# Pooled product gated in place, first pairs of the input and out projections in turns, VectorE's gates behind softmax scaling

## The reference

```python
h = rms_norm(x, norm_w)
proj = einsum('bld,dn->bln', h, w_in)      # 5824 columns: aq ak av ag bq bk bv bg cq ckv ckr cg du dg
ya = diff_attention(aq, ak, av, ...)       # 4 heads, two softmax maps per head, RMSNorm behind it
yb = axial_gqa(bq, bk, bv, ...)            # 4 query heads, 2 key heads
yc = latent_attention(cq, ckv, ckr, ...)   # cq and ckv normalised, then projected up
yd = multiscale_pool(du, w_group, scale)   # mean window minus token, per-group matmul, scale
y = concat(ya * silu(ag), yb * silu(bg), yc * silu(cg), yd * silu(dg))
x = x + einsum('bln,nd->bld', y, w_out)
```

## Time and profile before

| what | value |
|---|---|
| median of 3 runs | 952.94 us (951.38 to 953.1) |
| the profiled execution's own time | 950.87 us |
| its span | 948.8 us, 18299 instructions |
| TensorE matmul busy | 920.9 us (97%), 7138 instructions |
| TensorE weight load busy | 875.5 us (92%) |
| VectorE busy | 702.4 us (74%), 1130 instructions |
| ScalarE busy | 556.5 us (59%), 985 instructions |
| mean granted clock of TensorE | 0.994 |
| DMA | 143.97 MB, mean 152 GB/s |

### The profile page before, as it was taken

The page is one execution under the profiler, slowest core; times in us unless marked ns, Lnnn a source line. Parts: engine busy times, 40 slices in busy tenths (PEclk is TensorE's granted clock), DMA queues, the critical chain, the costliest instruction groups (busy, mean ns, idle before and its releaser), DMA issues.

```text
span 948.8 us, 18299 instructions
## 1 busy us (share of the span) xinstructions
PE 920.9 (97%) x7138; PEld 875.5 (92%) x7138; DVE 702.4 (74%) x1130; ACT 556.5 (59%) x985; POOL 0.2 (0%) x4
## 2 busy tenths in 40 slices
PE   8989999999999999999999989999999999989998
PEld 7988889998999998899999979999989998988998
DVE  7767987778797788876664568877787868787553
ACT  7667657658666565554544576666576565553331
POOL 0000000000000000000000000000000000000000
PEclk9999999999999999999999999999999999999999
DMA  9534332333333333245454343324334344335552
GB/s 357 224 127 181 131 133 90 135 133 134 134 134 136 132 134 133 89 179 178 179 189 179 134 178 134 134 102 166 134 134 178 115 154 159 138 111 200 194 177 90
DMA packets 22997, 143.97 MB, mean 152 GB/s; under 512 B 2560, under 2 KB 4608, under 8 KB 6528
## 3 DMA queue, kind: packets, MB, share of 16 engines
q1 hardware_dynamic: 22768, 142.77, 41.6%
q10 hardware_dynamic: 144, 0.04, 0.0%
HBM read 140.70 MB, written 2.10 MB: 151 GB/s over the span
## 4 chain that ended last, share of the span: by engine, by line
PE 73%; DVE 18%; ACT 7%; issue 2%; DMA 0%; ACTq 0%; DVEq 0%; SPq 0%
PE dense L671 21%; PE dense L673 21%; PE dense L672 21%; DVE w_lo L1250 5%; DVE c_st L1375 4%; PE o_ps L864 3%; PE s_ps L829 2%; ACT w_hi L954 2%; PE norm_ps L782 1%; PE t_ps L845 1%; DVE stat L1410 1%; ACT y_hi L1079 1%; ACT row L979 1%; DVE c_st L1374 1%; DVE row L1258 1%
## 5 line engine op out<-in xcount | busy, mean ns | idle before, releaser
L671 PE MATMUL dense<-h_hi,w_hi 128*128 128x272 f32 (+1 forms) x1472 | 438.3, 298 | 3.6 <-ACT row L979 1.8
L673 PE MATMUL dense<-h_hi,w_lo 128*128 128x272 f32 (+1 forms) x1472 | 422.6, 287 | 0.0
L672 PE MATMUL dense<-h_lo,w_hi 128*128 128x272 f32 (+1 forms) x1472 | 420.5, 286 | 0.0
L1250 DVE TENSOR_TENSOR w_lo<-raw,w_hi 128x1024 fp32r<-128x1024 f32 (+1 forms) x257 | 313.3, 1219 | 68.3 <-ACT w_hi L954 60.8
L954 ACT ACTIVATE w_hi<-raw 128x1024 fp32r<-128x1024 f32 (+1 forms) x257 | 271.3, 1056 | 69.3 <-PE dense L673 58.8
L671 PEld LDWEIGHTS dense<-h_hi,w_hi 128*128 128x128 f32 x1472 | 277.3, 188 | 10.8 <-issue 3.8
L672 PEld LDWEIGHTS dense<-h_lo,w_hi 128*128 128x128 f32 x1472 | 277.7, 189 | 1.4
L673 PEld LDWEIGHTS dense<-h_hi,w_lo 128*128 128x128 f32 x1472 | 277.0, 188 | 0.0
L671 PE MATMUL dense<-y_hi,w_hi 128*128 128x272 f32 (+1 forms) x564 | 163.6, 290 | 11.2 <-ACT row L979 7.1
L673 PE MATMUL dense<-y_hi,w_lo 128*128 128x272 f32 (+1 forms) x564 | 162.4, 288 | 0.0
L672 PE MATMUL dense<-y_lo,w_hi 128*128 128x272 f32 (+1 forms) x564 | 162.1, 287 | 0.0
(11 more groups left out here) (134 smaller groups left out, 707.0 us busy)
## 6 DMA issues: line engine op xcount, KB each, us to landing
raw<-w_stream_dram SPq DMA_DIRECT2D x128, 1024.0 KB, 4.8
out_dram<-x SPq DMA_DIRECT2D x8, 256.0 KB, 6.5
x<-xt_dram SPq DMA_DIRECT2D x3, 544.0 KB, 7.9
raw<-w_stream_dram SPq DMA_DIRECT2D x3, 512.0 KB, 7.2
con<-consts_dram SPq DMA_DIRECT2D x1, 984.0 KB, 13.4
x<-xt_dram SPq DMA_DIRECT2D x2, 272.0 KB, 4.6
raw<-w_stream_dram SPq DMA_DIRECT2D x2, 256.0 KB, 4.4
d_w<-consts_dram SPq DMA_DIRECT2D x2, 256.0 KB, 8.2
```

Source lines behind the costliest of these rows:

```text
L671: nc.tensor.matmul(ps, whi, xhi, start=first, stop=False)
L672: nc.tensor.matmul(ps, whi, xlo, start=False, stop=False)
L673: return nc.tensor.matmul(ps, wlo, xhi, start=False, stop=last)
L1250: signal(nc.vector.tensor_tensor(w_lo[:, g % RING, 0:n], raw[:, e % RAW, CHUNK * half:CHUNK * half + n], w_hi[:, g % RING, 0:n].bitcast(F3 ...
```

## The change

Six edits, all in the order of work and in which buffer or bank it uses; the matmuls are the same in number and shape.

1. Input pairs 0 and 1 of layer 0 and out pairs 0 and 1 of both layers are taken in turns: chunk b of pair 0, chunk b of pair 1, then b + 1. Since four tiles are then open, the tiles of the second pair lie in other banks (`side`): `t_ps` and `o_ps` at the start, `norm_ps` and `swap_ps` in the out projection.
2. At the start, x block 2 is loaded behind weight chunk 3 and x block 3 behind the next weights; constants and tables go three entries later; `x_first` stages stand later in the lists; the three lambda stages go from slots 8 to 10 to slots 13 to 15.
3. The `dg` gate writes its product in place, `c_st[:, i]`, and its `y_split` goes one slot later, with other offsets (ScalarE 0.77 to 0.23, VectorE 1.284 to 0.284).
4. VectorE's `gate` offset goes from 0.336 to 0.6.
5. `y_split` of ckv goes one slot later, the three stages of `kr` too.
6. `x_out` of pair 0 comes three slots later, where the pair now ends; layer 1's first lifts wait for the splits of layer 0's gated rows instead of for the gates.

```diff
+def pair_end(layer, p):
+    return 6 + p if layer == 0 and p < 2 else pair_slot(p) + 3
+
+def out_end(n):
+    return pair_slot(N_PAIRS) + (6 + n if n < 2 else 4 * n + 3)
...
-  AT_SCALAR:  y_gate=0.77
+  AT_SCALAR:  y_gate=0.23
-  AT_VECTOR:  gate=0.336, y_gate=1.284
+  AT_VECTOR:  gate=0.6, y_gate=0.284
...
     for s in range(1, AHEAD + 1):
-        plan += [(-10 + s, 0, ("split", 0, s)), (-10 + s, 1, ("x_first", 0, s))]
+        plan.append((-10 + 2 * s, 0, ("split", 0, s)))
+    plan += [(-5, 0, ("x_first", 0, 1)), (-3, 0, ("x_first", 0, 2)), (2.9, 0, ("x_first", 0, 3))]
...
             for n, stage in enumerate(("lam_dot", "lam_exp", "lam_out")):
-                at(8 + n, (stage, l))
+                at(13 + n, (stage, l))
...
                     if kind == "dg":
-                        at(s, ("y_split", "gate", l, kind, i0 + j, j))
+                        at(s + 1, ("y_split", "gate", l, kind, i0 + j, j))
...
-            at(s + n + 2, ("y_split", "lat_fin", l, key))
-        at(s + 3, ("rope_pre", l, "kr", 0, None))
-        at(s + 4, ("rope_stat", l, "kr", 0))
-        at(s + 5, ("rope_fin", l, "kr", 0))
+            at(s + 2 + 2 * n, ("y_split", "lat_fin", l, key))
+        at(s + 4, ("rope_pre", l, "kr", 0, None))
+        at(s + 5, ("rope_stat", l, "kr", 0))
+        at(s + 6, ("rope_fin", l, "kr", 0))
...
-    def chunk_kind(s):
+    def chunk_kind(l, s):
+        if l == 0 and s < 8:
+            return "in", s % 2, s // 2
...
-            return ("out", *divmod(s - pair_slot(N_PAIRS), 4))
+            n = s - pair_slot(N_PAIRS)
+            return ("out", n % 2, n // 2) if n < 8 else ("out", *divmod(n, 4))
...
+    def bank_of(tile):
+        if tile in side:
+            l, j = side[tile]
+            return (t_ps, o_ps)[j] if l is None else (norm_ps, swap_ps)[j]
+        return dense[tile % 2]
...
-            if e == 2:
+            if e == 2:
+                sp.dma_start(x[:, 12:16, :], xt[:, 12:16, :]).then_inc(s_x[3], 16)
+            if e == 5:
                 sp.dma_start(con[:, 0:N_MATS], consts[:, 0:N_MATS]).then_inc(s_const, 16)
-            if e == 3:
+            if e == 6:
...
         def bank_for(tile):
-            if tile >= 2:
-                kind, n = freed_by[tile - 2]
+            if tile in side:
+                l, j = side[tile]
+                if l is None:
+                    pass
+                elif j == 0:
+                    pe.wait_ge(rn_ready, 1 + max(n for st, n in norm_order.items() if st[1] == l))
+                else:
+                    last = [st for st in swap_list if st[1] == l][-1]
+                    pe.wait_ge(takes_swap[last[0]], swap_taken_value(last))
+            elif tile >= 2:
+                before_it = tile - 2 if tile - 2 not in side else tile - 4
+                kind, n = freed_by[before_it]
                 pe.wait_ge(taken[kind], n)
-            return dense[tile % 2]
+            return bank_of(tile)
...
-            signal(nc.vector.tensor_tensor(yt[:, t0:L], ta[:, t0:L], c_st[:, i, t0:L], ALU.mult), gate_done, n)
+            signal(nc.vector.tensor_tensor(c_st[:, i, t0:L], ta[:, t0:L], c_st[:, i, t0:L], ALU.mult), gate_done, n)
```

More of the change, by code:

```diff
@@ L108 @@
                  y_split=0.205, xscale=0.283, sub_pre=0.439, x_out=0.55, p_out=0.56, gate=0.574, s_exp=0.579,
-                 lift=0.6, up_out=0.705, split=0.71, x_square=0.72, y_gate=0.77, lam_exp=0.793, v_out=1.297)
+                 lift=0.6, up_out=0.705, split=0.71, x_square=0.72, y_gate=0.23, lam_exp=0.793, v_out=1.297)
 AT_VECTOR = dict(sq_sum=0.2, rope_mid=0.25, s_max=-0.418, lam_dot=-0.35, sub_fin=-0.345, rope_fin=-0.34, lat_fin=0.055, head_out=0.17,
-                 y_split=0.19, pool=0.266, xscale=0.283, gate=0.336, s_scale=0.491, x_out=0.512, rescale=0.55,
-                 x_add=0.614, split=0.71, lam_out=0.82, y_gate=1.284)
+                 y_split=0.19, pool=0.266, xscale=0.283, gate=0.6, s_scale=0.491, x_out=0.512, rescale=0.55,
+                 x_add=0.614, split=0.71, lam_out=0.82, y_gate=0.284)
 MOVED = {("split", 1, 56): 0.54, ("lift", 1, 2, 1): 0.49, ("lift", 0, 22, 0): -0.39, ("split", 1, 102): 0.87,
@@ L148, in make_plan @@
         for p, (kind, i0) in enumerate(PAIRS):
-            end = g0 + pair_slot(p) + 3
+            end = g0 + pair_end(l, p)
             for j in (0, 1):
@@ L219, in make_plan @@
         for n in range(O_PAIRS):
-            at(g0 + pair_slot(N_PAIRS) + 4 * n + 3, ("x_out", l, n))
+            at(g0 + out_end(n), ("x_out", l, n))
     return [("setup", 0)] + [stage for _, _, stage in sorted(plan)]
@@ L379, in build @@
     n_taken = {"in": 0, "up": 0, "out": 0}
-    freed_by, tile_no = {}, {}
+    freed_by, tile_no, side = {}, {}, {}
     n_tile = 0
@@ L393, in build @@
                 tile_no[(l, *m)] = n_tile
+                if m[0] == "out" and m[1] == 1:
+                    side[n_tile] = (l, m[2])
+                if l == 0 and m[0] == "in" and m[1] == 1:
+                    side[n_tile] = (None, m[2])
                 freed_by[n_tile] = (m[0], n_taken[m[0]])
@@ L557, in y_tile @@
             r = rows_of("d", source[3])
-            return n, lambda y: y[:, r, t0:L], yt[:, t0:L], (gate_done, gate_no[source])
+            return n, lambda y: y[:, r, t0:L], c_st[:, source[3], t0:L], (gate_done, gate_no[source])
         _, b, h, i = score_steps(l)[source[2]]
@@ L962, in lift @@
                 if l:
-                    act.wait_ge(gate_done, gates_of_layer * l)
+                    act.wait_ge(y_ready, max(y_count[(l - 1, 3, i)] for i in range(4)))
                 if kind == "cqr" and j and l:
@@ L1505, in add @@
             n += 1
-        for p in range(N_PAIRS):
+        for b in range(KT // CK) if l == 0 else ():
+            for p in (0, 1):
+                a = OFF[PAIRS[p][0]]
+                add(wi[CK * b:CK * b + CK, :, a:a + 256])
+        for p in range(2 if l == 0 else 0, N_PAIRS):
             kind, i = PAIRS[p]
@@ L1529, in pack_weights @@
                 n += 1
-        for p in range(O_PAIRS):
-            for b in range(KT // CK):
-                k = CK * OUT_ORDER[b]
-                add(wo[k:k + CK, :, 256 * p:256 * p + 256])
+        for p, b in ([(p, b) for b in range(KT // CK) for p in (0, 1)]
+                     + [(p, b) for p in range(2, O_PAIRS) for b in range(KT // CK)]):
+            k = CK * OUT_ORDER[b]
+            add(wo[k:k + CK, :, 256 * p:256 * p + 256])
     return stream.reshape(DEPTH * ENTRIES, 128, 2 * CHUNK)
```

16 lines of the change are left out of this document (9 added, 7 removed).

## The result

| | before | after |
|---|---|---|
| median (executions) | 951.92 us (14) | 955.83 us (15) |
| lowest and highest | 950.97 to 954.31 | 954.08 to 958.87 |
| profiled execution, span | 950.87, 948.8 | 956.15, 954.2 |
| all idle time ahead of matmuls | 24.2 us | 27.7 us |

The account below looks back on a forecast made before the run. TensorE was taken as the bound, its matmuls in flight 920.9 of 948.8 us. Start -1.5, up projection -3.7, out projection -2.8, gates +4.4 gave -3.6: 947.3 us, 949.3 on the median's scale; range from 944.0 to 954.0.

Parts of the forecast that it names:

- the gates: VectorE's gates pass s_scale and s_max, so other stages come later: loss 4.4 us, bounds 1.8 gain to 6 loss.
- the out projection: Pairs in turns: the last gated row is needed later, y_lo and x_out stalls go: gain 2.8 us (2.3 to 2.8).
- The start: Input pairs in turns: second chunk starts at about 10.9, fifth at 20.4: gain 1.5 us (1.0 to 2.0).
- The up projection: First up chunks: one long stall becomes two, clock kept in one layer of two: gain 3.7 us (1.8 to 5.6).
- rival 2: Lower clock stays behind both up projection stalls: 951.2 us, no difference that can be told; chance 0.23.
- Slot 93: Layer 0: s_max ahead of the gate makes it end at 383.9, y_split, p_out and pv follow: loss 2.0 us.
- Slot 95: Layer 0: a lift goes ahead of the y_split, so the 1.84 us stall falls by 0.4.
- Slot 83: s_scale first leaves VectorE idle, delaying head_out, its split and the lift: loss 0.85 us layer 0, 1.15 layer 1.
- Slots 89 and 90 of layer 0: The 0.74 us p_turn stall goes, gate 89 ends 2.3 us later, the later lift gives back 0.75.
- rival 3: Gate stalls grow to 2.5 us (layer 0) and 3.1 (layer 1), each bringing the clock down: 955.0 us; chance 0.11.
- signs of being wrong: No longer pv stall in layer 0's slot 94, granted clock 1.00 throughout or new falls, or waits for w_lo.
- number 1: VectorE catches up, so the gates' loss of 4.4 us shrinks to 0: 945 us; chance 0.19.

Follow-up runs that it names:

- e1: The kernel after with edit 4 alone undone (VectorE's gate offset back at 0.336): 944.7 us, ratio 0.9923.
- e3: The kernel after with one gate, layer 0 slot 66, back at 0.336 on VectorE: 950.95 us, ratio 0.9987.
- e4: The kernel after without the two MOVED entries for the weight splits of slots 101 and 102 in layer 1: 952.42 us, ratio 0.9997.
- e9: e5 with the out projection's first two pairs one after the other, in the two dense banks: 946.13 us, ratio 0.993.
- e5: The kernel after with VectorE's gates at 0.336 and without the two MOVED entries for splits of slots 101 and 102: 942.09 us, ratio 0.9888.
- e10: e5 with edit 5 undone (ckv's split and kr's three stages back in their slots): 946.46 us, ratio 0.9942.
- e12: The kernel after with one gate, layer 0 slot 93 (dg, head 0), back at 0.336 on VectorE: 955.00 us, ratio 1.003.
- e6: e5 with VectorE's gate offset 0.5 instead of 0.336, behind softmax scaling but ahead of s_max: 944.63 us, ratio 0.9917.
- e2: The kernel before with edit 4 alone (VectorE's gate offset 0.6): 964.92 us, ratio 1.0132.
- e11: e5 with the gated product written to yt again instead of in place: 941.46 us, ratio 0.9887.
- e7: e5 with the split of the gated rows later, behind the copies of p (ScalarE 0.6, VectorE 0.65): 938.22 us, ratio 0.985.

## Why the prediction was wrong

The sign was wrong. The step that failed is the loss put on the gates, 4.4 us: the runs show 11.1 (e1), and 4.9 of it (e3) hang on a path that the forecast's list of places did not have. A second step failed too: the 2.8 us gain of the out projection counted no wait for `w_lo`, and that wait, with the clock behind it, cost 3.4 (e4). Step by step, with the shares of the two profiled executions:

| step | forecast | measured | from |
|---|---|---|---|
| start | -1.5 | -1.1 | slot 4 |
| up projection | -3.7 | -4.9 | slots 14 to 20, both layers |
| out projection | -2.8 | +0.5 | layer 0 -0.8, a small shift between the layers +0.2, layer 1 +1.0 |
| gates | +4.4 | +10.9 | layer 0 from slot 50 to 98 +7.8, layer 1 from 21 to 99 +3.0 |

**The start** was right within its bounds in size, but the fifth chunk came at 20.83, not 20.4. The second chunk came as forecast where TensorE ran at full pace (10.89 in e3, 10.90 in e9; the kernel after is told of in the last section). What came late was the third: 13.9 forecast, 14.20 to 14.38 in e1, e3, e4, e5 and e9, where in e4 it still waits for VectorE's `h_lo` (0.17 us). **The up projection** was right down to the stalls: 1.6 and 1.1 us forecast in layer 0, 1.48 and 0.95 measured, and 1.40 and 1.05 in layer 1. (By the forecast's own rows the 1.6 should read 1.45: 3.30 less the 1.85 us by which TensorE starts sooner.) Only the clock was judged too low: it stayed up in both layers, not in one, so rival 2 falls. e10 confirms the size by itself (4.4 us).

**The out projection** failed on "a whole chunk of pair 1 lies between", with nothing late next. The `y_lo` waits went. But I asked what was late next for `y` and the banks and not for the weights. The places of the splits of slots 101 and 102 came from two `MOVED` entries that I had in view; they were made for an order in which slot 100 waits for the gated row anyway. Their price is 3.4 us (e4). With them gone the turned order is worth 4.0 against e9 and 2.1 against before's own out projection, on either side of the forecast 2.8.

**The gates** are where the forecast fell. Place by place:

- Slots 66 and 67 of layer 0 were not in the list at all: +5.7 us in the profile, 4.9 by e3. I had followed a late gate to `y_split`, to `head_out` and to ScalarE's exponential, but only where a `p_out` or a stall lay near. I had not followed the second thing that a gate releases: the `row` buffer that the next pair's `lift` writes. In the trace of before the slack there was 0.2 us, so it could have been read. The clock behind the stall was not in the sum either.
- Slot 93: 2.0 us and a stall of 2.5 were forecast, 2.54 us was the stall, with +3.5 us between slots 94 and 96 since the clock fell with it, and +2.1 in e4, where it did not. The size was right for half a reason, so in part by luck. e12 shows that the gate of slot 93 makes 1.28 of it; e6 and e12 together put the rest down to gates that pass the scaling in the slots ahead, where my list said 0.
- Slot 95: -0.4 forecast, -3.0 in the two profiles. The stall of 1.84 us is 1.42 in e4 and 1.43 in e1: the forecast's 0.4 was right. The rest of the 3.0 is not the edit's. The 0.35 in the kernel after (and 0.36 in e3) stands only where the clock had fallen just ahead, and the fall that before has at 397 has gone.
- Slot 83: +0.85 and +1.15 forecast, +0.9 and +1.3 measured. The counting by VectorE's idle time held.
- Slots 89 and 90 of layer 0: nothing net forecast, +0.6 measured from slot 88 to 94. The `p_turn` stall went, and the later `lift` held slot 93 for 1.20 us.
- Slots 89 to 93 of layer 1: +1.15 forecast, +1.7 measured from slot 87 to 95; the `lift` of slot 91 is late too (1.47 us), the `pv` stall 2.62 instead of the 3.1 that rival 3 had.
- Slot 51: a gain of 0.35 forecast, +0.1 measured. The stall of 0.73 us only moved, to a wait of 0.84 us for `qw` at 214.24.

Of the forecast's signs of being wrong one came, a wait for `w_lo`. Of the rivals, number 1 (the gates cost nothing) falls with e1. Number 3 had the right kind of mechanism (late gates, longer stalls, new falls of the clock) and a time of 955.0, close to 955.83. That nearness is luck: its sum was two new falls (3.8 us) on a kernel 1.7 us faster than before, and the runs show another sum. Its places were only half right: slot 94 in two profiles (after, e3) and not in two others (e2, e4), 843.88 no fall in the profiled execution, and slot 66 missing. I held it at 0.11 because I took 3.3 us for the point at which the clock falls, from two stalls that did it and one that did not. The trace of before spoke against that point: the clock fell behind the 1.84 us stall of the earlier trace rows too (0.54 from 397 to 399).

The sum of what the runs show: edit 4 costs 11.1 us, the two kept `MOVED` entries 3.4, together 13.7 (e1, e4, e5). Against them stand 4.4 for edit 5 (e10), 4.0 for the turned out projection (e9), 1.1 at the start (profile alone, no run of its own), and 0 for the product in place (e11). That is 9.5 of the 10.3 us between before and e5 (952.40 - 942.09). With the 2.1 of the out projection against before in place of the 4.0 it is 7.6, and 2.7 have no run that shows their place. The two profiled executions themselves (950.87 and 942.65) lie 8.2 apart, and the same places make that up: 1.2 at the start, 5.0 in the up projections, 2.1 in the out projections. Also open: how the 6.2 us of edit 4 outside slot 66 divide; beside slot 66 only slot 93 was tried alone.

## What to carry to other kernels

In a list worked in strict order, a stage moved back by a quarter of a slot is late for everything that it releases, not only for its result: write down each semaphore that it raises and every waiter on it, buffers that it frees included, and read at each occurrence how much slack the waiter had. Single exceptions (`MOVED`) are made for one order; when the order changes, take them out first and see which still pay. And try the parts apart: without the two left-over exceptions five of the six edits were worth 10 us together; the sixth and the exceptions cost 14.

## What the hardware showed that I had not expected

The length of a stall does not say whether the clock falls behind it. It fell to 0.50 behind 1.43 us in e1, and not behind 2.02 us in the same execution; in e5, with both stalls as long, it fell behind both (0.50 from 392 to 394, 0.59 from 838 to 840). A stall of 3.31 us in e2, the one of the earlier trace rows, kept the clock (1.00 from 63 to 69). TensorE of e1, then its windows:

```profile
390.36 1.94 PE L903 MATMUL o_ps<-p_t,v_st 128*128 128x16 f32 x12 [1.43 <-ACT p_t L1169]
...
838.57 1.60 PE L903 MATMUL o_ps<-p_t,v_st 128*128 128x128 f32 x12 [2.02 <-ACT p_t L1169]
```
```profile
392.00:394.00 2.00, 2.00 (x10) 2.00 (x10) 1.54 (x3) 0.51 (x2) 0.00 (x0) 0.50 0.94 397
840.00:842.00 2.00, 2.00 (x19) 2.00 (x18) 1.36 (x3) 0.50 (x2) 0.00 (x0) 1.00 0.97 410
```

Nor does the place in the kernel: a stall of 2.62 us kept the clock in the kernel after (1.00 from 849 to 851), and one of 2.63 us, the same `pv` in e3, did not:

```profile
843.00:847.00 4.00, 4.00 (x21) 4.00 (x22) 1.73 (x3) 1.49 (x3) 0.00 (x0) 0.58 0.77 262
```

Two stalls of 1.48 and 0.95 us only 3.4 us apart kept it in all nine profiles that have edit 5 as it stands, in both layers. What decides between such cases no run here shows.

The falls are also most of the spread from run to run. The executions of the kernel after go from 954.08 us at a mean granted clock of 0.995 to 958.87 us at 0.987; those of e7, all at 1.000, lie within 0.5 us of each other. So one profile does not place a fall for good. e7 has lost every fall, and that is most of what its profile has over that of e5: 4.2 us, with 18.0 us of idle time ahead of matmuls against 18.7, and no fall against two.

The row of granted clock does not show every slow stretch. In the profiled execution of the kernel after the matmuls of the first chunk start 0.227 us apart until 10.7, as they do at 0.50 behind 277; in e1's they start 0.126 apart. The clock reads 1.00 in both. The window of the kernel after, then that of e1:

```profile
8.00:10.00 2.00, 2.00 (x10) 2.00 (x10) 1.50 (x4) 1.55 (x2) 0.00 (x0) 1.00 1.03 407
8.00:10.00 2.00, 1.83 (x15) 1.64 (x14) 1.35 (x4) 1.46 (x2) 0.00 (x0) 1.00 1.02 415
```

So the second chunk began at 11.75 there and at 11.00 in e1, and the fifth at 20.83 and 20.81 all the same. The profiles of e2, which starts as before does, and of e10, which starts as the kernel after does, have the slow first chunk too; what decides it no run shows.
